# A mixture-of-experts encoder: expert weights in six transfers of 1 MB instead of twelve of 0.5 MB

## The reference, cut to what matters

```python
for i in range(DEPTH):
    h = rmsnorm(x, norm_mix_g[i])
    x = x + (sgu_mixer(h, ...) if i % 2 == 0 else pool_mixer(h, ...))
    h = rmsnorm(x, norm_ffn_g[i])
    x = x + hierarchical_moe(h, ...)
return rmsnorm(x, final_norm_g)

def expert_block(args):            # 128 rows of one expert
    xb, e = args
    hid = jax.nn.silu(xb @ w_gate[e]) * (xb @ w_up[e])
    return hid @ w_down[e]
```

## Time and profile before

| | us |
|---|---|
| median of three runs | 2259.09 |
| lowest and highest | 2257.99, 2264.34 |
| profiled execution, first to last instruction (span) | 2255.5 |
| PE busy | 2009.1 (89%) |
| PE weight loads busy | 1662.5 (74%) |
| DVE busy | 1592.5 (71%) |
| ACT busy | 1365.6 (61%) |
| POOL busy | 336.2 (15%) |
| DMA, over the span | 553.90 MB, 246 GB/s |

### The profile page before, as it was taken

One profiled execution on the slowest core, in us unless ns is written; L12 is line 12 of the kernel. 1 busy time (PEld: TensorE's weight loads), 2 busy tenths in 40 slices (PEclk: granted clock), 3 DMA queues, 4 the chain that ended last, 5 costly groups with the idle time before them and its releaser, 6 DMA issues.

```text
span 2255.5 us, 32390 instructions
## 1 busy us (share of the span) xinstructions
PE 2009.1 (89%) x9356; PEld 1662.5 (74%) x9356; DVE 1592.5 (71%) x1887; ACT 1365.6 (61%) x1746; POOL 336.2 (15%) x338
## 2 busy tenths in 40 slices
PE   7999999999829999999999579896499999999980
PEld 5887878887717888888887468675388888878870
DVE  3335343443558999999998676747599999889875
ACT  3442233522417888888888533434288888888872
POOL 1000000000031111212211230001311121122214
PEclk9999999999959999999999879998699999999995
DMA  7231223322536999999999642116489999999966
GB/s 266 94 97 62 94 94 101 94 75 85 192 122 226 378 381 382 379 388 372 380 380 366 243 173 93 57 65 252 127 295 374 382 377 380 379 365 381 386 255 231
DMA packets 165993, 553.90 MB, mean 246 GB/s; under 512 B 31525, under 2 KB 33733, under 8 KB 163760
## 3 DMA queue, kind: packets, MB, share of 16 engines
q1 hardware_dynamic: 139728, 511.99, 61.6%
q0 software_dynamic: 26208, 41.19, 5.3%
HBM read 540.57 MB, written 47.78 MB: 261 GB/s over the span
## 4 chain that ended last, share of the span: by engine, by line
PE 39%; DMA 33%; issue 11%; DVE 9%; POOLq 3%; POOL 3%; ACT 1%; DVEq 0%; SPq 0%; ACTq 0%
DMA y_rows<-big,metas 19%; PE bank L486 13%; PE bank L487 12%; PE bank L488 12%; DMA metas<-lists 12%; POOLq L426 2%; DVE big L981 2%; POOL lists L416 1%; POOL big L437 1%; DVE a_lo L970 1%; DVE bank L1071 1%; PE bank L500 1%; DVE x_res L996 1%; DMA big<-normed,metas 1%; DMA big<-y_rows 1%
## 5 line engine op out<-in xcount | busy, mean ns | idle before, releaser
L486 PE MATMUL bank<-w_hi,a_hi 128*128 128x512 f32 x1816 | 727.5, 401 | 26.2 <-DVE a_lo L970 15.9
L488 PE MATMUL bank<-w_hi,a_lo 128*128 128x512 f32 x1816 | 713.4, 393 | 0.0
L487 PE MATMUL bank<-w_lo,a_hi 128*128 128x512 f32 x1816 | 712.5, 392 | 0.0
L970 DVE TENSOR_TENSOR w_lo<-raw,w_hi 128x1024 fp32r<-128x1024 f32 x384 | 456.9, 1221 | 349.6 <-ACT w_hi L716 348.3
L716 ACT ACTIVATE w_hi<-raw 128x1024 fp32r<-128x1024 f32 x384 | 405.8, 1061 | 465.9 <-PE bank L488 458.2
L970 DVE TENSOR_TENSOR w_lo<-big,w_hi 128x1024 fp32r<-128x1024 f32 x522 | 612.6, 1221 | 45.8 <-ACT w_hi L716 30.1
L716 ACT ACTIVATE w_hi<-big 128x1024 fp32r<-128x1024 f32 x522 | 536.5, 1064 | 72.4 <-PE bank L488 62.8
L486 PEld LDWEIGHTS bank<-w_hi,a_hi 128*128 128x128 f32 x1816 | 345.1, 190 | 104.0 <-issue 22.6
L488 PEld LDWEIGHTS bank<-w_hi,a_lo 128*128 128x128 f32 x1816 | 343.8, 189 | 74.2
L487 PEld LDWEIGHTS bank<-w_lo,a_hi 128*128 128x128 f32 x1816 | 344.6, 190 | 67.3
L970 DVE TENSOR_TENSOR a_lo<-bank,a_hi 128x512 fp32r<-128x512 f32 x263 | 170.1, 684 | 106.6 <-ACT a_hi L716 106.6
(11 more groups left out here) (140 smaller groups left out, 1646.9 us busy)
## 6 DMA issues: line engine op xcount, KB each, us to landing
big<-in_w_down SPq DMA_DIRECT2D x260, 512.0 KB, 7.2
big<-in_w_up SPq DMA_DIRECT2D x254, 512.0 KB, 6.8
raw<-in_w_gate SPq DMA_DIRECT2D x252, 512.0 KB
raw<-in_a_w_in SPq DMA_DIRECT2D x64, 512.0 KB, 4.0
raw<-in_a_w_out SPq DMA_DIRECT2D x32, 512.0 KB, 3.2
big<-y_rows SPq DMA_DIRECT2D x16, 1024.0 KB, 6.5
normed<-big SPq DMA_DIRECT2D x4, 2048.0 KB, 9.3
raw<-in_b_w_in SPq DMA_DIRECT2D x16, 512.0 KB, 3.5
```

What stands on the lines that cost most here:

```text
L486: pe.matmul(dst, left_hi, right_hi, start=first, stop=False)
L487: pe.matmul(dst, left_hi, right_lo, start=False, stop=False)
L488: return pe.matmul(dst, left_lo, right_hi, start=False, stop=last)
L970: return nc.vector.tensor_tensor(dst, src, f32(hi), ALU.subtract)
```

## The change

A pair of neighbouring units is one transfer of 1 MB, 8 KB per partition. The views of the pairs (`moe_pair`) lie over the same places. `M.raw` has six semaphores instead of twelve, and SP waits until the second unit of a pair has been split before it refills both. ACT waits, for either unit of a pair, until the pair has landed. Item 1 keeps its places: its gate is two pairs, the first half of up stays two transfers of 0.5 MB (one in `big`, one in `spatial`, with a semaphore `raw_odd`), the second half of up is a pair in `vbias`. Nothing is changed for PE, DVE and POOL. The diff, cut:

```diff
+        moe_pair = [raw[:, 2 * n:2 * n + 2, :].rearrange("p s f -> p (s f)") for n in range(RING // 2)] + \
+                   [bu[:, 2 * n * UNIT:2 * (n + 1) * UNIT] for n in range((ROUND - RING) // 2)]
+        early_pair = [bv[:, 0:2 * UNIT], bv[:, 2 * UNIT:4 * UNIT], None, vbias[:, 0:2 * UNIT]]
+        GP, DP = GU // 2, DN // 2
...
-        m = [sems(f"moe{n}", MOE, {"raw": ROUND, "stored": HALVES}) for n in range(LAYERS)]
+        m = [sems(f"moe{n}", MOE, {"raw": ROUND // 2, "stored": HALVES}) for n in range(LAYERS)]
...
-                def load_gu(e, j, slots=moe_raw):
-                    w = gate if j < DN else up
-                    k = 2 * (j % DN)
-                    sp.dma_start(slots[j].rearrange("p (e k f) -> p e k f", e=1, k=2),
-                                 w[:, bass.ds(e, 1), k:k + 2, :]).then_inc(M.raw[j], 16)
+                def load_gu(e, m, pairs=moe_pair):
+                    w = gate if m < GP // 2 else up
+                    k = 4 * (m % (GP // 2))
+                    sp.dma_start(pairs[m].rearrange("p (e k f) -> p e k f", e=1, k=4),
+                                 w[:, bass.ds(e, 1), k:k + 4, :]).then_inc(M.raw[m], 16)
+
+                def load_dn(e, m, pairs=moe_pair[GP:]):
+                    sp.dma_start(pairs[m].rearrange("p (e k d) -> p e k d", e=1, k=2),
+                                 down[:, bass.ds(e, 1), 2 * m:2 * m + 2, :]).then_inc(M.raw[GP + m], 16)
...
+                sp.wait_ge(M.stored[0], 16)
+                sp.wait_ge(M.logits, 1)
+                for m_ in range(2):
+                    sp.wait_ge(M.raw[m_], 16)
+                    load_gu(1, m_, early_pair)
+                sp.wait_ge(M.stored[1], 16)
+                sp.wait_ge(M.logits, 3)
+                sp.wait_ge(M.raw[2], 16)
+                sp.dma_start(early_raw[4].rearrange("p (e k f) -> p e k f", e=1, k=2), up[:, 1:2, 0:2, :]) \
+                    .then_inc(M.raw[2], 16)
+                sp.wait_ge(M.rw_lo, 1)
+                sp.dma_start(early_raw[5].rearrange("p (e k f) -> p e k f", e=1, k=2), up[:, 1:2, 2:4, :]) \
+                    .then_inc(M.raw_odd, 16)
+                item_2(range(RING // 2))
+                sp.wait_ge(M.table, 1)
+                sp.wait_ge(M.raw[3], 16)
+                load_gu(1, 3, early_pair)
+                item_2(range(RING // 2, GP))
...
                 with sp.Fori(4, n) as i:
...
-                    for j in range(GU):
-                        sp.wait_ge(M.lo, ROUND * (i - 1) + j + 1)
-                        load_gu(e_up, j)
-                    for j in range(DN):
-                        sp.wait_ge(M.lo, ROUND * (i - 1) + GU + j + 1)
-                        load_dn(e_dn, j)
+                    for m_ in range(GP):
+                        sp.wait_ge(M.lo, ROUND * (i - 1) + 2 * m_ + 2)
+                        load_gu(e_up, m_)
+                    for m_ in range(DP):
+                        sp.wait_ge(M.lo, ROUND * (i - 1) + GU + 2 * m_ + 2)
+                        load_dn(e_dn, m_)
...
                 def unit(c, loads, used, gap=0, slots=moe_raw):
-                    act.wait_ge(M.raw[c], 16 * loads)
+                    act.wait_ge(M.raw[c // 2], 16 * loads)
+                    if slots is early_raw and c == 5:
+                        act.wait_ge(M.raw_odd, 16)
```

More of the change, by code:

```diff
@@ L185, in encoder_trunk @@
                "h_full", "h_hi", "h_lo", "y_out", "meta_s", "scattered",
-               "added", "small", "summed"]
-        m = [sems(f"moe{n}", MOE, {"raw": ROUND, "stored": HALVES}) for n in range(LAYERS)]
+               "added", "small", "summed", "raw_odd"]
+        m = [sems(f"moe{n}", MOE, {"raw": ROUND // 2, "stored": HALVES}) for n in range(LAYERS)]
         SU = 3 * 2 * KC
@@ L242, in moe @@
                 down = A["w_down"][L].rearrange("e (p k) d -> p e k d", k=DN)
-                def load_gu(e, j, slots=moe_raw):
-                    w = gate if j < DN else up
-                    k = 2 * (j % DN)
-                    sp.dma_start(slots[j].rearrange("p (e k f) -> p e k f", e=1, k=2),
-                                 w[:, bass.ds(e, 1), k:k + 2, :]).then_inc(M.raw[j], 16)
-                def load_dn(e, j, slot=None):
-                    sp.dma_start((slot if slot is not None else moe_raw[GU + j]).rearrange("p (e k d) -> p e k d", e=1, k=1),
-                                 down[:, bass.ds(e, 1), j:j + 1, :]).then_inc(M.raw[GU + j], 16)
+                def load_gu(e, m, pairs=moe_pair):
[6 more added lines that the diff above has]
+                                 down[:, bass.ds(e, 1), 2 * m:2 * m + 2, :]).then_inc(M.raw[GP + m], 16)
                 before_lo(sp)
-                for j in range(RING):
-                    load_gu(0, j)
+                for m_ in range(RING // 2):
+                    load_gu(0, m_)
                 before_y(sp)
-                for j in range(RING, GU):
-                    load_gu(0, j)
-                for j in range(DN):
-                    load_dn(0, j)
+                for m_ in range(RING // 2, GP):
+                    load_gu(0, m_)
+                for m_ in range(DP):
+                    load_dn(0, m_)
                 for h in range(HALVES):
@@ L266, in moe @@
                                  hn[h]).then_inc(M.stored[h], 16)
[L268 to L297, removed]
-                for j in range(GU):
-                    sp.wait_ge(M.lo, 2 * ROUND + j + 1)
-                    load_gu(3, j)
+                def item_2(pairs):
+                    for m_ in pairs:
+                        sp.wait_ge(M.lo, 2 * m_ + 2)
+                        sp.wait_ge(M.raw[m_], 32)
+                        load_gu(2, m_)
@@ new lines, in moe @@
+                sp.wait_ge(M.rw_lo, 1)
[6 more added lines that the diff above has]
+                item_2(range(RING // 2, GP))
+                for m_ in range(DP):
+                    sp.wait_ge(M.lo, ROUND + 2 * m_ + 2)
+                    sp.wait_ge(M.raw[GP + m_], 16)
+                    load_dn(1, m_, early_pair)
@@ L301, in moe @@
+                for m_ in range(DP):
+                    sp.wait_ge(M.lo, ROUND + GU + 2 * m_ + 2)
+                    sp.wait_ge(M.raw[GP + m_], 32)
+                    load_dn(2, m_)
+                for m_ in range(GP):
+                    sp.wait_ge(M.lo, 2 * ROUND + 2 * m_ + 2)
+                    load_gu(3, m_)
                 n = sp.value_load(table[0:1, 0, TABLE - 1:TABLE], min_val=E - 2, max_val=ITEMS_MAX - 2) + 2
@@ L304, in moe @@
                     e_dn = sp.value_load(table[0:1, 0, bass.ds(i - 1, 1)], min_val=0, max_val=E - 1)
-                    for j in range(GU):
-                        sp.wait_ge(M.lo, ROUND * (i - 1) + j + 1)
-                        load_gu(e_up, j)
-                    for j in range(DN):
-                        sp.wait_ge(M.lo, ROUND * (i - 1) + GU + j + 1)
-                        load_dn(e_dn, j)
+                    for m_ in range(GP):
+                        sp.wait_ge(M.lo, ROUND * (i - 1) + 2 * m_ + 2)
+                        load_gu(e_up, m_)
+                    for m_ in range(DP):
+                        sp.wait_ge(M.lo, ROUND * (i - 1) + GU + 2 * m_ + 2)
+                        load_dn(e_dn, m_)
                 e_dn = sp.value_load(table[0:1, 0, bass.ds(n - 1, 1)], min_val=0, max_val=E - 1)
-                for j in range(DN):
-                    sp.wait_ge(M.lo, ROUND * (n - 1) + GU + j + 1)
-                    load_dn(e_dn, j)
+                for m_ in range(DP):
+                    sp.wait_ge(M.lo, ROUND * (n - 1) + GU + 2 * m_ + 2)
+                    load_dn(e_dn, m_)
                 next_weights()
```

## The result

| | before | after |
|---|---|---|
| median of the runs, us | 2261.72 (2257.99 to 2283.63, 4 runs) | 2331.68 (2323.03 to 2350.99, 4 runs) |
| ratio | 1 | 1.031, 95% interval 1.026 to 1.036 |
| span of the profiled execution, us | 2255.5 | 2331.5 |

What follows compares the result with a forecast made beforehand. POOL's serial chain of small DMAs, as long as PE's item, was taken as the bound. +73 us for POOL's turns and +2 us for the tails on 2255.5 gave 2330.5, plus 3.6 to the median: 2334 us; range 2247 to 2470 us.

Steps and rivals of the forecast that it cites:

- The bound: Expert loops: POOL's serial chain of small DMAs, 17.70 us a turn, is as long as PE's item and has no slack.
- Edit 1, packets: Weight loads: pairs move as 8 KB packets, 48 instead of 96 per engine and item, -0.5 us of engine time.
- Edit 2, POOL's turns: POOL's chain: each turn waits for at most one larger SP packet, +0.15 us; in sum +1.2 us per item, +73 us.
- Edit 3, deeper queues: Queueing before POOL's DMAs: +6.5 us per item if engines hold a fixed number of packets, 0 if bytes; 0 taken.
- Edit 4, refill in pairs: Weight refill in the loops: a pair's first unit comes 2.6 us later, covered by over 6 us of slack: 0 us.
- Edit 5: SP and the ramp: six issues and six waits fewer per item, early loads keep their order and places: 0 us.
- Edit 6, the tail: End of each layer: one more copy behind the last down pair's landing, +1 us per layer, +2 us.
- Faster (batching pays): Expert loops: larger transfers shorten the backlog and the list lands in time, at best -12 us, 2247 us; chance 0.15.
- No change: Expert loops: POOL's longer waits are absorbed, or rows are cut to 4 KB packets: 2259 us, give or take 7; chance 0.12.
- Much slower: POOL's DMAs: queues counted in packets, 2730 us in full, more likely 2470 to 2535 us; chance 0.10 beyond 2470 us.

Runs made afterwards that it cites:

- delayed kernel: The kernel before, with POOL clearing a free tile after each scatter has landed and waiting for it; weights and packets untouched: 2358.18 us, ratio 1.0417.
- the two kernels with 4 KB packets: The changed kernel with 4 KB rows, refilled in pairs: as 1 MB transfers 2285.17 us, ratio 1.0063; as two 0.5 MB transfers per pair 2273.1 us, 1.0037.
- POOL's reordering: POOL loads the next gather's list while the scatter still lands: on the kernel before 2241.46 us, ratio 0.988; on the changed kernel 2250.23 us, 0.9915.

## Why the prediction was right

- *The bound.* It named POOL's chain of small DMAs. Shown from both sides: shorter, the kernel falls to PE's floor; longer by 1.0 us, it loses 93 us; with slack, 8 KB packets cost 9 us and the delay 4.5 us.
- *Edit 1, packets.* 8 KB packets came as read from the loads of `y_rows`.
- *Edit 2, POOL's turns.* The sum was +1.2 us per item. Measured: 1.26 us in the two waits, 1.56 in the turn of layer 0, 1.35 in the items of both layers. The total holds; parts of it do not. I took 0.2 us off because SP's ring would be emptier when PE stalls. The delayed kernel shows the reverse. Over 760 to 1150 us its POOL waits 134.3 us in 20 turns for the scatter and 82.6 us in 16 for the list: 6.72 + 0.96 (the memset) + 1.36 + 5.16 = 14.2 us, against 7.62 + 5.11 = 12.7 us before. That is 1.5 us for the 1.0 us that was put in, with no change of packets. Why is open. A burst of ACT after a stall (999.94, four units in one go) does not explain it, since the kernel before has such fours without a stall:

```profile
908.73 4.03 ACT L716 ACTIVATE w_hi<-big 128x1024 fp32r<-128x1024 f32 x4
```

And the pace does not follow the chain one for one on average: stalls vary (up to 6 us), and a long one costs clock. So the packets themselves probably added less than 1.2 us to the chain in the loop, and the way the loop runs when late added the rest. That each of POOL's packets waits for one packet of SP's was inferred from equal counts in 2 us, some nine packets on each engine. The sizes of the landings fit it, and no run isolates it.
- *Edit 3, deeper queues.* 0 us taken. The lists' landings, with two turns each, went from 4.8 and 5.2 us to 5.1 and 5.4 us in the loops: +0.3 and +0.2 us, what two turns make (0.3), and a small part of the 2.7 us that a doubled queue would add. At PE's pace the list grew by 1.1 us, where a doubled queue would add some 3. So the lists speak against a fixed number of packets held ahead; the scatter's +2.4 us there does not, since doubling its queueing would add 6.3 - 3.26 = 3.0 us.
- *Edit 4, refill in pairs.* This term was wrong: not 0 but 8 to 20 us, by the two kernels with 4 KB packets. The cover I named, ACT's slack of 6 us, held. The cost came another way that I had not listed. The range took it up.
- *Luck in the total.* 2334 us forecast and 2332 measured agree better than their parts. The packets by themselves are worth 2.5%, about 56 us and not 73; the pairs, forecast at nothing, fill the gap.
- *Edit 5* holds as far as the profile shows it: the first scatter of layer 0 comes at 710.3 us, before at 713.0. *Edit 6, the tail*: two copies stand behind each landing; in the first tail ACT waits 3.09 and 0.77 us for `in_w_down`, and the tail is 0.5 us longer, not 1. In the medians so little cannot be told.
- *Rivals.* Faster (batching pays): excluded by the time. The engines did not even need less of it for the bytes: SP's queue took 93.3% for 12.61 MB before and 85.0% for 11.21 MB after, 7.4 and 7.6% per MB. At PE's pace it is 7.2% with either packet (91.6% for 12.67 MB, 91.7% for 12.82 MB). No change: excluded by the time, and the 8 KB packets are in the counts. Much slower: excluded by the time.

## What to carry to other kernels

Find the serial chain of small DMAs and compare its length with the pace of the busiest engine. Where they are equal, the row length of every other transfer lengthens it: 8 KB rows instead of 4 KB cost 2.5% here. That this is because the queues share an engine packet by packet fits the counts and is not isolated. Cut the chain first (here by issuing the next load under a landing that is waited for anyway); the size of the bulk transfers then hardly matters (9 us of 2250 here). And a kernel that looks bound by a fully busy PE can still lose a microsecond per item to a delay of the same size on the least busy engine.

## What the runs showed of the hardware

Time of a packet on its engine: 0.16 us for 4 KB and 0.31 for 8 KB in stretches where SP's queue had the engines to itself, so that 8 KB rows save 3 to 4% there. In the loops, from 842 to 878 us, beside POOL's packets: 0.093 us for 2 KB, 0.175 for 4 KB (93.3%, 12.61 MB), 0.36 for 8 KB (85.0%, 11.21 MB). So 2 KB rows cost some 7% more engine time than 4 KB rows there, and 8 KB rows saved nothing.

A list of 2 KB took 4.8 to 5.2 us (medians) to land beside a stream of weights in 4 KB packets. With POOL's reordering and PE at its pace, a scatter landed in 6.3 us beside 4 KB packets and in 8.7 us beside 8 KB packets refilled in pairs.

After a stall of 5.3 us PE ran its next matmuls 0.43 us apart, at the lower clock level, and then 0.23 us apart; the delayed kernel had a mean granted clock of 0.939 where before had 0.951.
